# Expert results scattered by choice and token, the last two blocks mixed in by TensorE, and the up product split throughout

## What is computed

```python
g_sel = argmax(h @ w_rg + b_rg)                  # 1 group of 4
top_v, top_i = top_k(e_logits of that group, 2)  # 2 experts of its 8
w2 = softmax(top_v) * p_sel
out = zeros_like(h)
for n in range(32):
    a, b = split(h @ w_up[n], 2)                 # 1024 -> 2 x 256
    out += combine[:, n:n+1] * ((silu(a) * b) @ w_down[n])   # 256 -> 1024
x = x + out
```

## Time and profile before

| | us |
|---|---|
| median of three executions | 2645.57 |
| profiled execution | 2643.07 |
| its span | 2641.10 |
| TensorE busy | 2495.4 (94%) |
| VectorE busy | 1587.7 (60%) |
| ScalarE busy | 1145.1 (43%) |
| GpSimd busy | 235.7 (9%) |

### The profile page before, as it was taken

The page is one execution under the profiler, slowest core; times in us unless marked ns, Lnnn a source line. Parts: engine busy times, 40 slices in busy tenths (PEclk is TensorE's granted clock), DMA queues, the critical chain, the costliest instruction groups (busy, mean ns, idle before and its releaser), DMA issues. The chain is left out here.

```text
span 2641.1 us, 32353 instructions
## 1 busy us (share of the span) xinstructions
PE 2495.4 (94%) x11409; PEld 1903.3 (72%) x11409; DVE 1587.7 (60%) x2386; ACT 1145.1 (43%) x1898; POOL 235.7 (9%) x237
## 2 busy tenths in 40 slices
PE   8999997799999999999999999999899899999995
PEld 6877785577888886766788888678757677666663
DVE  6766445745555525644655553548899656588784
ACT  5423332434444324623444442433333532377773
POOL 0000001000000000000000000345424000111111
PEclk9999999999999999999999999999999999999997
DMA  4321231032333321202233331322202004599995
GB/s 150 108 84 64 96 112 56 31 138 80 96 95 95 128 104 53 86 33 82 93 96 96 97 141 49 111 98 85 95 32 96 1 33 133 184 371 377 387 390 200
DMA packets 196720, 320.65 MB, mean 121 GB/s; under 512 B 16513, under 2 KB 112673, under 8 KB 196609
## 3 DMA queue, kind: packets, MB, share of 16 engines
q1 hardware_dynamic: 191678, 310.71, 34.1%
q0 software_dynamic: 4736, 8.40, 1.0%
q10 hardware_dynamic: 195, 0.06, 0.0%
HBM read 298.43 MB, written 29.10 MB: 124 GB/s over the span
## 5 line engine op out<-in xcount | busy, mean ns | idle before, releaser
L399 PE MATMUL ps<-ffn_parts 128*128 128x512 f32 x1056 | 411.6, 390 | 2.4 <-DVE ffn_parts L394 1.7
L401 PE MATMUL ps<-ffn_parts 128*128 128x512 f32 x1056 | 410.9, 389 | 0.0
L400 PE MATMUL ps<-ffn_parts 128*128 128x512 f32 x1056 | 410.8, 389 | 0.0
L399 PEld LDWEIGHTS ps<-ffn_parts 128*128 128x128 f32 x1056 | 198.2, 188 | 46.5 <-issue 2.6
L394 DVE TENSOR_TENSOR ffn_parts<-ring,ffn_parts 128x1024 fp32r<-128x1024 f32 x132 | 157.7, 1222 | 117.9 <-ACT ffn_parts L2454 107.4
L401 PEld LDWEIGHTS ps<-ffn_parts 128*128 128x128 f32 x1056 | 198.2, 188 | 41.3
L400 PEld LDWEIGHTS ps<-ffn_parts 128*128 128x128 f32 x1056 | 198.2, 188 | 40.9
L394 POOL TENSOR_TENSOR w_lo<-ring,w_hi 128x512 fp32r<-128x512 f32 (+1 forms) x112 | 161.0, 1442 | 720.8 <-ACT w_hi L558 720.4
L2505 DVE SCALAR_TENSOR_TENSOR y_tmp<-ps,pcol,y_tmp 128x511 f32<-128x511 f32 x88 | 61.9, 745 | 214.0 <-ACT y_tmp L2438 214.0
L1012 ACT CAST front_w_hi<-ring 128x512 fp32r<-128x512 f32 x104 | 64.1, 620 | 214.1 <-PE ps L401 214.0
L394 DVE TENSOR_TENSOR front_w_lo<-ring,front_w_hi 128x512 fp32r<-128x512 f32 x104 | 71.5, 688 | 131.5 <-ACT front_w_hi L1012 131.3
(11 more groups left out here) (666 smaller groups left out, 5561.9 us busy)
## 6 DMA issues: line engine op xcount, KB each, us to landing
ring<-in_w_up SPq DMA_DIRECT2D x32, 1536.0 KB, 9.4
ring<-in_ffn_w_up SPq DMA_DIRECT2D x88, 512.0 KB, 5.0
moe_down<-in_w_down SPq DMA_DIRECT2D x32, 1024.0 KB, 10.5
ring<-in_ab_w_in SPq DMA_DIRECT2D x13, 2048.0 KB, 7.9
ring<-in_w_in SPq DMA_DIRECT2D x11, 2048.0 KB, 7.8
ring<-in_ffn_w_down SPq DMA_DIRECT2D x10, 2048.0 KB, 7.7
ring<-in_w_up SPq DMA_DIRECT2D x32, 512.0 KB, 10.2
ring<-in_c_w_in SPq DMA_DIRECT2D x6, 2048.0 KB, 8.1
```

What stands on the lines that cost most here:

```text
L399: nc.tensor.matmul(out, left[0], right[0], start=start, stop=False, **more)
L400: nc.tensor.matmul(out, left[0], right[1], start=False, stop=False, **more)
L401: return nc.tensor.matmul(out, left[1], right[0], start=False, stop=stop, **more)
```

## The change

1. `WHOLE` is gone: all eight up tiles are split, in four parts of two tiles. TensorE's plain f32 products and VectorE's x copy go; each block has six more products, one more cast (ScalarE) and one more rest (VectorE). The up weights still come in two DMAs, now six tiles and the last two.
2. The DRAM tensor of results has one row per choice and token (1024 rows, `results_of_choices`). GpSimd scatters each block's results there by index (L4129 of the changed kernel, an indirect DMA that leaves out slots without a token) in place of SyncE's store. The indices come from eight small products on TensorE (`results`), like the token indices.
3. SyncE loads the results in order, 128 tokens of one choice per DMA (L4105), when all blocks but the last two are scattered and the ring is free.
4. The last two blocks are not stored. Their results, weighted (`last_result` on ScalarE, `split_result` on VectorE), are split and multiplied with one-hot matrices of slot and token by TensorE (`mixed`, 32 products), and VectorE adds that from PSUM (`add_mixed`). For it the shares of those slots are moved by eight small products. VectorE computes the shares after block 3 (`shares_of_blocks`).
5. There is no second block of code: additions and stores follow in the same programs.

```diff
-WHOLE = 2
-SPLITS = (KD - WHOLE) // 2
-SPLIT_ROWS, WHOLE_ROWS = slice(0, SPLITS), slice(SPLITS, KD // 2)
+SPLITS = KD // 2
+FIRST_ROWS, LAST_ROWS = slice(0, SPLITS - 1), slice(SPLITS - 1, SPLITS)
...
             def step(n):          # sync
                 more = inside(n, 2)
                 if more:
                     expert = expert_of(later(n, 2))
+                    sp.wait_ge(e.up_split, at_block(n, SPLITS, SPLITS - 1))
+                    load_up(later(n, 2), expert, FIRST_ROWS, e.up_loaded)
+                if more:
                     sp.wait_ge(e.up_split, at_block(n, SPLITS, SPLITS))
-                    load_up(later(n, 2), expert, SPLIT_ROWS, e.up_loaded)
-                if inside(n, -2):
-                    store(later(n, -2))
-                if more:
-                    sp.wait_ge(e.whole_done, at_block(n, 1, 1))
-                    load_up(later(n, 2), expert, WHOLE_ROWS, e.whole_loaded)
+                    load_up(later(n, 2), expert, LAST_ROWS, e.last_loaded)
                     sp.wait_ge(e.down_split, at_block(n, 1, 1))
                     load_down(later(n, 2), expert)
...
-            store((before, 2, 4))
-            store((before, 3, 4))
+            for t in range(NT):
+                if t % 2 == 0:
+                    sp.wait_ge(*r.ring_free(t // 2 + 1))
+                for s in range(2):
+                    at = s * T + t * P
+                    sp.dma_start(picked[:, 2 * t + s, :], y_dram[at:at + P, :]).then_inc(r.row_picked[2 * t + s], 16)
+            for t in range(NT):
+                sp.wait_ge(*r.combined(t + 1))
+                sp.dma_start(tiles[:, t, :], k.x[:, t, :]).then_inc(k.param_loaded.sem, 16)
...
+            def scatter(n, index):          # gpsimd
+                nc.gpsimd.indirect_dma_start(y_dram, bass.IndirectOffsetOnAxis(ap=index, axis=0), e.y[0:ROWS, side(n), :], None, bounds_check=2 * T - 1, oob_is_err=False)\
+                    .then_inc(e.y_stored[side(n)], 16)
+            def free_ring():
+                for s in range(2):
+                    pool.wait_ge(e.y_stored[s], pairs_before((before, 6, 8)))
+                for n in ((before, 6, 8), (before, 7, 8)):
+                    pool.wait_ge(e.up_split, at_block(n, SPLITS, SPLITS))
+                    nc.gpsimd.sem_inc(r.ring_free.sem, 1)
...
             def first(n):          # tensor
                 pe.wait_ge(e.x_ready, at_block(n, 1, 1))
-                pe.wait_ge(e.whole_loaded[s], pair(n, 16))
-                for c in range(WHOLE):
-                    last = nc.tensor.matmul(out, e.x_whole[:, s, c, :], up[s][:, KD - WHOLE + c, :], start=(c == 0), stop=False)
-                last.then_inc(e.whole_done, 1)
                 for q in range(SPLITS):
...
+            def mixed(t, b, half):
+                out, at = k.ps[:, MIXED[t] + half, :], slice(half * BANK, (half + 1) * BANK)
+                for n, y in enumerate((e.dn_hi, e.dn_lo)):
+                    last = nc.tensor.matmul(out, at_slot(b)[:, t * P:(t + 1) * P], y[0:ROWS, 0, b, at], start=(b == 0 and n == 0), stop=(b == 1 and n == 1),
+                                            skip_group_check=True)
...
+            def last_result(b, n):          # scalar
+                act.wait_ge(*r.shares_read(1))
+                act.wait_ge(e.down_done, at_block(n, 1, 1))
+                for half in range(2):
+                    at = slice(half * BANK, (half + 1) * BANK)
+                    nc.scalar.activation(e.dn_hi[0:ROWS, 0, b, at], k.ps[0:ROWS, (YB, XB)[b] + half, :], ACT.Copy, scale=r.share_of_slot[0:ROWS, b:b + 1]).then_inc(r.results_cast.sem, 1)
...
             each_block(dve, before, step, after)          # vector
-            rows_and_shares(k, r, dve)
+            add_picked(0, (0, 1))
+            add_picked(1, (0,))
+            split_result(1)
+            add_picked(1, (1,))
+            add_picked(2, (0, 1))
+            add_mixed(0)
+            add_picked(3, (0, 1))
+            for t in range(1, NT):
+                add_mixed(t)
```

More of the change, by code:

```diff
@@ L3989, in rows_and_shares @@
     nc.vector.tensor_tensor(r.share2[:, :, :], r.share2[:, :, :], r.share1[:, :, :], ALU.mult)
+    dve.drain()
+    shares = r.shares[:, :, 0]
+    for out, block, relation in ((r.share_of_last[:, :, 0], 0, ALU.is_equal), (r.share_of_last[:, :, 1], 1, ALU.is_equal), (r.share_before[:, :], 0, ALU.is_lt)):
+        nc.vector.scalar_tensor_tensor(out=out, in0=r.block[:, :], scalar=r.last[:, block:block + 1], in1=shares, op0=relation, op1=ALU.mult)
+    dve.drain()
+    nc.vector.tensor_copy(r.share_parts[:, :, 0:2], r.share_of_last[:, :, :])
+    dve.drain()
+    nc.vector.tensor_tensor(r.share_parts[:, :, 2:4], r.share_of_last[:, :, :], r.share_parts[:, :, 0:2], ALU.subtract).then_inc(r.shares_split.sem, 1)
 def at_block(n, times=1, more=0):
@@ L4007, in experts @@
     XB, UB, YB, HB = 0, 2, 4, 6
+    MIXED = (2, 6, 4, 0)
+    tiles = out.rearrange("o (t p) d -> p (o t) d", p=P)
     def side(n):
@@ L4145, in _ @@
             after(3)
-            before = pair_before_last(nc.gpsimd)
-            each_block(pool, before, lambda n: step(n) if isinstance(n, tuple) or n >= 4 else None, lambda n: after(n) if n > 3 else None, STATIC_ROWS)
+            for n in range(4, STATIC_ROWS):
+                step(n)
+                hand_out(n - 4)
+                after(n)
+            before = nc.gpsimd.value_load(r.before_last[0:1, 1:2], min_val=NE // 2 - 4, max_val=NB // 2 - 4)
+            with pool.Fori(STATIC_ROWS // 2 - 2, NB // 2 - 3) as i:
+                with pool.If(i <= before):
+                    for b in range(2):
+                        step((i, 4 + b, 0))
+                        hand_out((i, b, 0))
+            for b in range(2):
+                step((before, 6 + b, 8))
+                hand_out((before, 2 + b, 8))
+            for b in range(2):
+                hand_out((before, 4 + b, 8))
+            free_ring()
             pool.drain()
@@ L4173, in first @@
                     for c in (2 * q, 2 * q + 1):
-                        last = product(nc, out, [x[:, s, c, :] for x in (e.x_hi, e.x_lo)], [w[:, c, :] for w in (e.up_hi, e.up_lo)], False, c == 2 * SPLITS - 1)
+                        last = product(nc, out, [x[:, s, c, :] for x in (e.x_hi, e.x_lo)], [w[:, c, :] for w in (e.up_hi, e.up_lo)], c == 0, c == 2 * SPLITS - 1)
                     last.then_inc(e.up_done, 1)
@@ L4189, in second @@
                 pe.wait_ge(e.hid_split, at_block(n, 1, 1))
-                if not early(n, 1):
+                bank = YB
+                if isinstance(n, tuple) and n[1:] == (3, 4):
+                    bank = XB
+                    pe.wait_ge(*r.shares_read(1))
+                elif not early(n, 1):
                     pe.wait_ge(e.y_ready, at_block(n))
@@ L4235, in in_blocks_beyond, with results @@
                 pe.wait_ge(*r.slotted(3))
+            def results(out, early, late):
+                for t in range(2 * NT):
+                    last = nc.tensor.matmul(out, r.is_slot[:, t, :], early[:, t, :] if t < NT else late[:, t - NT, :], start=(t == 0), stop=(t == 2 * NT - 1), skip_group_check=True)
+                last.then_inc(r.results_found.sem, 1)
             def after(n):
@@ L4239, in after, with shares_of_slots @@
                     tokens(NBANKS - 1, MORE, in_blocks_beyond, r.token_of_block)
+                    results(k.ps[0:ROWS, NBANKS - 1, MORE:2 * MORE], r.result_of_block, r.result_of_block[:, NT:2 * NT, :])
+            def shares_of_slots():
+                pe.wait_ge(*r.shares_split(1))
+                for t in range(2 * NT):
+                    last = nc.tensor.matmul(k.ps[0:ROWS, XB, 0:4], r.is_slot[:, t, :], r.share_parts[:, t, :], start=(t == 0), stop=(t == 2 * NT - 1))
+                last.then_inc(r.shares_moved.sem, 1)
+            def mixed(t, b, half):
[3 more added lines that the diff above has]
+                                            skip_group_check=True)
+                if b == 1 and half == 1:
+                    last.then_inc(r.mixed.sem, 1)
             fill_wait(k, NBANKS - 1, 4)
@@ L4257, in _ @@
             turn_hidden(0)
+            pe.wait_ge(*r.results_read(1))
             each_block(pe, before, step, after)
+            pe.wait_ge(*r.results_split(2))
+            for t in range(NT - 1):
+                for half in range(2):
+                    mixed(t, 0, half)
+            for half in range(2):
+                pe.wait_ge(*r.results_split(3 + half))
+                mixed(0, 1, half)
+            for t in range(1, NT):
+                for b in ((1,) if t < NT - 1 else (0, 1)):
+                    for half in range(2):
+                        mixed(t, b, half)
         @block.scalar
@@ L4317, in step @@
                     silu(later(n, 1))
+                if last_but_one(n):
+                    split_hidden(later(n, 1))
+                    last_result(0, n)
+                    last_result(1, later(n, 1))
+                    return
```

(2 more changed lines are left out.)

187 lines of the change are left out of this document (110 added, 77 removed).

## The result

| | before | after |
|---|---|---|
| median, four runs each on one chip | 2645.82 | 2697.30 |
| lowest to highest | 2643.05 to 2646.64 | 2696.04 to 2702.20 |
| span of a profiled execution | 2641.10 | 2695.5 |

The change made the kernel slower, by about 2%: ratio 1.020, 95% interval 1.0188 to 1.0213. The forecast was 2625.5, its range 2619 to 2637 with its first rival. It was wrong in sign.

A forecast was written before the change was run, and what follows sets the result against it. TensorE was taken to set the pace, DMA near the edge. Span 2641.10 less 8.2 (to A) and 10.2 (end) is 2622.7; plus 1.97, 2624.7; with half of 2.5, 2625.5. Range 2619 to 2631, to 2637 with rival 1.

The forecast's parts named there:

- rival 1: Expert loop: VectorE and ScalarE pace it, the period stays at 9.50, the time is 2635.5; chance 0.15.
- stores and scatters: GpSimd in the loop: twice the copy and indirect issue per block, busy 26.70 of 230 us before; DMA share 0.99.
- Rival 4: GpSimd in the loop: a scatter holds the queue and delays the next gather; about 2654 at 8 us per scatter; chance 0.04.
- The split: Up product of each block: TensorE gains 0.33, period 9.50 to 9.17; 31 blocks give 10.2 us less.
- rival 2: Expert loop: DMA paces it, 9.3 per block, 4 us more, 2629.5; chance 0.10.
- The end: From the last hidden turn in the loop to the span's end: 36.3 for 46.5 before, gain 10.2.
- Rivals 3 and 5: End: result loads come late, 2629 to 2632, chance 0.09; or early loading doesn't take place, near 2634, chance 0.04.
- the work among the first blocks: Added small products and VectorE bookkeeping in the first blocks: +2.0 us, bounds 0.8 and 7.4.
- the routing ahead of the first block: Eight more small products where TensorE waits for the gather, and GpSimd's longer numbering: 0.
- A: Anchor at the last hidden turn inside the loop, 2594.56 before; forecast to come 8.2 us early.

The follow-up runs named there:

- kernel with 28 static blocks: Changed kernel with both index copies behind one drain, and GpSimd's indices at fixed places up to row block 28 of 32: 2628.84, ratio to before 0.9935.
- the kernel before with stamps: Kernel before, with a copy, a drain, a second copy and a second drain on GpSimd behind every gather of the loop: 2645.66, one run.
- the two lines exchanged: Changed kernel with GpSimd scattering block n's result before gathering the later block's rows, both drains kept: 2709.32, ratio to before 1.024.

## Why the prediction was wrong

**The step that failed** is the last sentence on stores and scatters: "A scatter waits for the result, and the next gather is queued behind it, but that gather has some two periods to its use." It priced GpSimd by its busy time (twice the copy and the indirect issue) and never named the two drains in that queue. The number to price them was at hand, the gather's landing of 6.4. With the drain as a wait for landing, the first block of the timeline takes 7.5 (gather to scatter) and 3.4 (scatter to gather), 10.9, and the second 12.6 (gathers at 2441.38 and 2452.26, the next at 2464.88); once the row turns are late the gathers are 10.9 to 13.9 apart. Measured over the last 22 of the row periods it is 12.19, against 9.19 in the kernel with 28 static blocks: 66 us. The lead of the gathers was real, but it is used up once: in the changed kernel the first late row turn comes at 2399.60, with the third gather of the loop.

**Rival 4** named the place (GpSimd's order gather, scatter, gather, and the gather late) and had 0.04. It named the wrong price: a long issue of the scatter, deciding from 7 us each. The issue took 0.94. Its 2654 assumed 8 us per scatter; the loss was larger. The reason for so low a chance was that the rows showed gathers of about 1 us each; those rows say what an issue costs, not what a drain behind it waits for.

**What held:**
- The split. 9.19 to 9.17 a block for 9.17 forecast; at the measured 0.31 to 0.33 per block it is worth 9.5 to 10.2 (10.2 forecast). VectorE at 92.7 and ScalarE at 89.0 of 100 us hide their added work, so rival 1 was wrong.
- DMA. Forecast share 0.99, measured 0.99, and rival 2 was wrong as well: with a share of 1.02 the split alone ran at 9.17.
- The end. Forecast 36.3, measured 36.7 and (with 28 static blocks) 36.1; before 46.5. Rivals 3 and 5 were wrong.

**What was mis-sized:** the work among the first blocks. Over eight periods the kernel with one drain and 28 static blocks took 78.05 (2299.98 to 2378.03), eight of 9.19 are 73.5: 4.5 against 1.0 before, so +3.5 for the +2.0 taken. The kernel with the split alone had 2.0 more than before already; that VectorE, with little time to spare, falls behind there fits, but was not tried by itself. And the routing ahead of the first block, priced at nothing, takes 1.1 longer: from ScalarE's first cast of the expert part to the first row turn 17.4 before, 18.5 in the changed kernel and 18.4 with the split alone.

**Slips in the sum.** Half of 2.5 added to 2624.7 is 2625.9, not 2625.5, and the addition said to begin at 2635.31 is the last but one (the row has two). Neither changes the outcome.

With the drains out of the way the sum closes: from the first row turn to A 298.74 before and 293.24 after, 5.5 less, where 31 x 0.31 - 3.5 give 6.1; the end 10.4 less. The execution shown before had its first row turn 4.2 earlier (2295.82 against 2299.98), 3.0 of it at the start of the expert part already and 1.1 in the routing; the 3.0 are no cost of the change, for the kernel before with stamps, which is the same program up to there, is 3.1 later too in its first looped copy, 2357.89 against 2354.78. So spans differ by 11.8 and medians by 16.6. At 2628.84 the change is inside the forecast's own range of 2619 to 2631: that is about what it is worth with the drains off the path.

## What to carry to other kernels

Walk through the queue of every engine to which a DMA issue is added, and list what stands between two issues: a drain or any other wait for completion costs the landing of what was issued before it, not an issue. Sum the landings around the ring of that queue and hold the sum against the period; if it is larger, order doesn't help and the lead of prefetched data only delays the loss. Put the small copies that need a drain side by side behind one drain, at a point where the DMAs before it have had time to land (one drain in the loop still waited 1.0 to 5.6 here), or give the indices fixed places so that none is needed.

## What the runs showed of the hardware

- A drain on GpSimd waits for the landing of an indirect DMA issued before it: a scatter held by it starts 0.84 us after TensorE has seen the gather's landing (2448.00 and 2448.84, 2460.60 and 2461.44, and 15 times more in that loop); with nothing under way the drain cost 0.85 behind its copy. The profile calls the wait "issue", so an "issue" of several microseconds on GpSimd is worth a look at the code.
- Two indirect DMAs without a drain between them are under way together: in the blocks written out a scatter was issued 3.9 us after a gather, and in the kernel with 28 static blocks such gathers land in 5.6 (median).
- A scatter (32 rows with a token on average: 1024 choices over 32 blocks) landed in 2.8 us with no gather under way (median with the two lines exchanged) and 6.6 beside gathers and a DMA share of 0.99.
- A GpSimd copy of 96 integers from SBUF to SBUF took 0.17 to 1.24 us as a rule, and 6.56, 6.58 and 6.70 in three kernels, each ending with an unbroken run of VectorE's two-input operations.
- With TensorE waiting 33.8 us in 14 of 16 blocks for gathered rows, the mean granted clock was 0.90, so TensorE was at its lower level, 1.2 GHz, for part of the time: after some of the stops eight row turns took up to 1.54 us instead of 0.82, and the products behind them stood 0.43 apart instead of 0.23 (2462.36 to 2464.06). TensorE was busy for 169.2 of these 200 us, some 10.4 a block of 12.3, where a block without stops takes 9.19: the stops cost more than their length.
